# Expert picks in a two-block transformer kernel: the gathered dense part turned around on TensorE, and its masked sums moved from VectorE to TensorE

## What is computed

```python
experts = (i1 * PEER_N_KEYS + i2).reshape(T, PEER_HEADS * PEER_TOPK)
gates = jax.nn.softmax(top_vals, axis=-1).reshape(T, PEER_HEADS * PEER_TOPK)
...
u = jnp.take(expert_down, ec, axis=0)
hdn = jax.nn.gelu(jnp.einsum('ted,td->te', u, xc))
vsel = jnp.take(expert_up, ec, axis=0)
return jnp.einsum('te,ted->td', gc * hdn, vsel)
```

## Time and profile before

| what | value |
|---|---|
| median of 3 runs | 3120.47 us (3116.56 to 3124.34) |
| the profiled execution | 3122.72 us |
| its span | 3120.9 us |
| TensorE busy | 2909.6 us (93%) |
| VectorE busy | 2118.9 us (68%) |
| ScalarE busy | 1105.1 us (35%) |
| GpSimd busy | 557.2 us (18%) |
| DMA | 803.77 MB, 258 GB/s on average |
| expert stage | about 1900 us to the end |
| dense down products | 1900.2 to 2287 us |
| down rows | 1912.5 to 2576.7 us |
| tile-0 builds | from 2394 us |
| dense up products | 2651.4 to 3066 us |
| up rows | 2577.8 to 3104 us |

### The profile page before, as it was taken

One profiled execution on the slowest core, in us unless ns is written; L12 is line 12 of the kernel. 1 busy time (PEld: TensorE's weight loads), 2 busy tenths in 40 slices (PEclk: granted clock), 3 DMA queues, 4 the chain that ended last, 5 costly groups with the idle time before them and its releaser, 6 DMA issues.

```text
span 3120.9 us, 40850 instructions
## 1 busy us (share of the span) xinstructions
PE 2909.6 (93%) x16091; PEld 2422.2 (78%) x16091; DVE 2118.9 (68%) x3183; ACT 1105.1 (35%) x1716; POOL 557.2 (18%) x524
## 2 busy tenths in 40 slices
PE   7999999999999999899999999999987669999992
PEld 7999999997879987798887799888876657444441
DVE  5777777777765456744545658985578989666667
ACT  2334443444354444544444542111146757000000
POOL 0000000000000000000000002234333556544444
PEclk9899999999999999999999999999999968999996
DMA  9977777777866534465333546999966888999998
GB/s 333 338 249 255 266 259 256 261 254 239 292 199 170 156 115 148 136 197 157 114 108 114 179 159 236 316 346 407 403 245 202 276 274 302 396 410 410 410 409 308
DMA packets 359295, 803.77 MB, mean 258 GB/s; under 512 B 40152, under 2 KB 99920, under 8 KB 358336
## 3 DMA queue, kind: packets, MB, share of 16 engines
q1 hardware_dynamic: 284480, 502.08, 47.5%
q0 software_dynamic: 74624, 299.07, 25.9%
HBM read 798.96 MB, written 2.10 MB: 257 GB/s over the span
## 4 chain that ended last, share of the span: by engine, by line
PE 55%; DMA 20%; DVE 15%; issue 4%; POOL 3%; ACT 2%; SPq 0%; DVEq 0%; ACTq 0%; POOLq 0%
PE ps L1972 15%; PE ps L1974 15%; PE ps L1973 15%; DMA s<-in_up_rows,s 11%; DMA s<-in_down_rows,s 8%; DVE s L1915 5%; POOL s L701 3%; DVE s L1937 2%; PE ps L2397 1%; DVE s L1880 1%; PE ps L2016 1%; PE ps L2265 1%; DVE r L1202 1%; DMA s<-in_ada_w 1%; DVE s L1883 1%
## 5 line engine op out<-in xcount | busy, mean ns | idle before, releaser
L1972 PE MATMUL ps<-r,r 128*128 128x256 f32 (+1 forms) x3232 | 1049.6, 325 | 2.2 <-DVE r L1202 1.8
L1974 PE MATMUL ps<-r,r 128*128 128x256 f32 (+1 forms) x3232 | 1029.1, 318 | 0.0
L1973 PE MATMUL ps<-r,r 128*128 128x256 f32 (+1 forms) x3232 | 1029.0, 318 | 0.0
L1202 DVE TENSOR_TENSOR r<-s,r 128x1024 fp32r<-128x1024 f32 (+2 forms) x532 | 640.4, 1212 | 510.6 <-ACT r L716 510.2
L716 ACT CAST r<-s 128x1024 fp32r<-128x1024 f32 (+2 forms) x532 | 549.4, 1039 | 842.9 <-PE ps L1974 779.9
L1972 PEld LDWEIGHTS ps<-r,r 128*128 128x128 f32 x3232 | 622.8, 193 | 50.0 <-issue 9.2
L1973 PEld LDWEIGHTS ps<-r,r 128*128 128x128 f32 x3232 | 623.0, 193 | 43.5 <-issue 4.6
L1974 PEld LDWEIGHTS ps<-r,r 128*128 128x128 f32 x3232 | 622.0, 192 | 41.1
L1937 DVE SCALAR_TENSOR_TENSOR s<-s,s,s 128x1088 f32<-128x1088 f32 x256 | 345.8, 1351 | 162.0 <-DMA s<-in_up_rows,s 157.9
L1915 DVE CUSTOM_DVE_ANT_0 s<-s,s 128x1152 f32<-128x1152 f32 x256 | 345.0, 1353 | 108.8 <-DMA s<-in_down_rows,s 108.4
L2630 PE MATMUL ps<-s,big 128*128 128x480 f32 x1024 | 414.6, 568 | 0.0
(11 more groups left out here) (300 smaller groups left out, 2492.4 us busy)
## 6 DMA issues: line engine op xcount, KB each, us to landing
s<-in_ada_w SPq DMA_DIRECT2D x192, 512.0 KB, 5.7
s<-in_ret_w_in SPq DMA_DIRECT2D x128, 512.0 KB, 5.2
s<-in_up_blocks SPq DMA_DIRECT2D x128, 480.0 KB, 6.8
s<-in_down_blocks SPq DMA_DIRECT2D x128, 448.0 KB, 6.5
s<-in_w_in SPq DMA_DIRECT2D x96, 512.0 KB, 3.8
s<-in_ret_w_in SPq DMA_DIRECT2D x128, 256.0 KB, 4.0
s<-in_ret_w_out SPq DMA_DIRECT2D x64, 512.0 KB, 5.7
s<-in_mla_w_in SPq DMA_DIRECT2D x48, 512.0 KB, 3.7
```

Of the source, the lines that this page charges most:

```text
L1202: v.tensor_tensor(lo_of(w), raw_of(w), hi_of(w).bitcast(F), ALU.subtract).then_inc(*lo_made.to(w))
L1972: pe.matmul(o, lh, rh, start=start, stop=False, skip_group_check=True)
L1973: pe.matmul(o, lh, rl, start=False, stop=False, skip_group_check=True)
L1974: return pe.matmul(o, ll, rh, start=False, stop=stop, skip_group_check=True)
```

## The change

- DH is laid out as (i1, token) instead of four parts of (token, 32 of i1), so the dense copy is contiguous.
- `pick_rows` swaps the sides: the dense part of a token is stationary, with a step of 256 elements between its 128 columns, and PH moves. The result has i1 on partitions and the picks along the row.
- The comparison becomes four products that put the picks' i1 on all partitions, and VectorE compares them with the partition number (`POS`, a new column of the table). In tile 0 the banks 0 and 1 alternate for it; in tile 1 it is bank 1.
- The sum over i1 is now over partitions: `add_picked` makes four width-1 products of PR with a column of ones, into bank 5. The VectorE sum is gone. ScalarE copies the whole tile's sums once (`sums_copy`).
- PR has three buffers instead of two, at a new place.
- The row numbers of picks and masks change; the masks 29 to 31 of tile 0 go behind row 255, around `hidden(1)` and `coefficients(1)`.

```diff
-        PR = [sbuf[0][i][:, 0:512] for i in (2, 3)]
+        PR = [at(W + 4608 + 512 * i, 512) for i in range(3)]
...
-        PICK_AT = [146 + q // 2 for q in range(32)] + [164 + 5 * q // 2 for q in range(32)]
-        HOT_AT = [163 + 5 * (q + 3) // 2 for q in range(32)]
+        PICK_AT = [146 + 5 * q // 4 for q in range(32)] + [187 + 2 * q for q in range(32)]
+        HOT_AT = [194 + 2 * q for q in range(28)] + [251]
...
-                s.copy(DH[:, i1 // 32, :, i1 % 32:i1 % 32 + 2], bank[4 + q % 4].rearrange("p (i t) -> p t i", i=2)).then_inc(
-                    *hid_stored.to(q))
+                s.copy(flat(DH[:, i1:i1 + 2, :]), bank[4 + q % 4]).then_inc(*hid_stored.to(q))
...
-                v.scalar_tensor_tensor(out=o, in0=bank[1], scalar=0.0, in1=o, op0=ALU.is_equal,
+                v.scalar_tensor_tensor(out=o, in0=bank[1 if t else q % 2], scalar=POS, in1=o, op0=ALU.is_equal,
                                        op1=ALU.mult).then_inc(*multiplied.to((t, q)))
-                v.wait_ge(*multiplied.at((t, q)))
-                v.tensor_reduce(SL[t][:, 4 * q:4 * q + 4], o.rearrange("p (t i) -> p t i", t=4), AX.X, ALU.add).then_inc(
-                    *picked.to((t, q)))
...
             def pick_rows(t, q):
-                b = 3 + q % 2
+                b, b1 = 3 + q % 2, 1 if t else q % 2
                 take(b)
                 pe.wait_ge(*pick_hot.at((t, q)))
                 for k in range(4):
-                    c = 128 * t + 4 * q + k
-                    pe.matmul(bank[b][:, k * 128:(k + 1) * 128].rearrange("p (c i) -> p c i", c=4), PH[q % 2][:, k, :],
-                              DH[:, :, c, :], start=True, stop=True)
-                less(t, q, 0, 1).then_inc(*rows_picked.to((t, q)))
-                free[1], free[b] = multiplied.at((t, q)), rows_copied.at((t, q))
+                    pe.matmul(bank[b][:, k * 128:(k + 1) * 128], DH[:, :, 128 * t + 4 * q + k], PH[q % 2][:, k, :],
+                              start=True, stop=True)
+                take(b1)
+                for k in range(4):
+                    r = pe.matmul(bank[b1][:, k * 128:(k + 1) * 128], IDR[:, 4 * q + k:4 * q + k + 1].broadcast_to([128, 128]),
+                                  EFR[t][:, 0, :], start=True, stop=True)
+                r.then_inc(*rows_picked.to((t, q)))
+                free[b1], free[b] = multiplied.at((t, q)), rows_copied.at((t, q))
+
+            def add_picked(t, q):
+
+                pe.wait_ge(*multiplied.at((t, q)))
+                for k in range(4):
+                    r = pe.matmul(SUMS[t][:, 4 * q + k:4 * q + k + 1], PR[(32 * t + q) % 3][:, k * 128:(k + 1) * 128],
+                                  ONES[:, 0:1], start=True, stop=True)
+                r.then_inc(*picked.to((t, q)))
...
             for q in range(32):
                 if q < 31:
                     spread_(0, q + 1)
+                if q >= 2:
+                    add_picked(0, q - 2)
                 pick_rows(0, q)
             spread_(1, 0)
+            add_picked(0, 30)
...
+            first_ones(0, 29)
+            hidden(1)
+            first_ones(0, 30)
+            add_row(0)
+            first_ones(0, 31)
+            coefficients(1)
+            add_row(1)
+            add_row(2)
+            for n in range(3, 256):
+                add_row(n)
+                if n < 35:
+                    first_ones(1, n - 3)
```

More of the change, by code:

```diff
@@ L38 @@
 K_NEG = 2066
-K_ALL = 2067
+K_POS = 2067
+K_ALL = 2068
 def tables():
@@ L294, in build @@
         SQE = at(16 * KB, G2C)
-        PR = [sbuf[0][i][:, 0:512] for i in (2, 3)]
-        CO = [big.rearrange("p (c h i t) -> p c h i t", c=4, h=2, i=32)[:, :, t, :, :] for t in range(2)]
+        PR = [at(W + 4608 + 512 * i, 512) for i in range(3)]
+        CO = [DH[:, :, 128 * t:128 * (t + 1)] for t in range(2)]
         def row_slot(n):
@@ L572, in build @@
         spread, spread_read, pick_hot = sig("spread", fours), sig("spread_read", fours), sig("pick_hot", fours)
-        rows_picked, rows_copied = sig("rows_picked", fours), sig("rows_copied", fours)
+        rows_picked = sig("rows_picked", fours)
+        rows_copied = sig("rows_copied", fours[:33] + [("sum", 0)] + fours[33:] + [("sum", 1)])
         multiplied, picked = sig("multiplied", fours), sig("picked", fours)
@@ L583, in build @@
         last_root, last_made = sig("last_root", range(2)), sig("last_made", range(2))
+        SUMS = [bank[5][:, 128 * t + 128:128 * t + 256] for t in range(2)]
         BANK_OF = {(x, p): 4 + p % 2 if x == "N0" else (6, 7, 0, 1)[p] if x == "C" else p for x, p in pairs}
@@ L1104, in rows_copy, with sums_copy @@
                 s.wait_ge(*rows_picked.at((t, q)))
-                if 32 * t + q >= 2:
-                    s.wait_ge(*picked.at(fours[32 * t + q - 2]))
-                s.copy(PR[q % 2], bank[3 + q % 2]).then_inc(*rows_copied.to((t, q)))
+                if 32 * t + q >= 3:
+                    s.wait_ge(*picked.at(fours[32 * t + q - 3]))
+                s.copy(PR[(32 * t + q) % 3], bank[3 + q % 2]).then_inc(*rows_copied.to((t, q)))
+            def sums_copy(t):
+                s.wait_ge(*picked.at((t, 31)))
+                s.copy(SL[t], SUMS[t]).then_inc(*rows_copied.to(("sum", t)))
             def store(t, q):
                 s.wait_ge(*built.at((t, q)))
-                s.copy(CO[t][:, :, :, 4 * q:4 * q + 4], bank[6 + q % 2].rearrange("p (t c i) -> p c i t", t=4, c=4)).then_inc(
+                s.copy(CO[t][:, :, 4 * q:4 * q + 4], bank[6 + q % 2].rearrange("p (t i) -> p i t", t=4)).then_inc(
                     *stored.to((t, q)))
@@ L1119, in coefficients @@
                 s.wait_ge(*coef_turned.at(t))
-                s.copy(CFT[t], bank[5][:, 0:128]).then_inc(*coef_copied.to(t))
+                s.copy(CFT[t], bank[5 * t][:, 0:128]).then_inc(*coef_copied.to(t))
             def first_tile(q):
@@ L1155, in scalar @@
                 if q == 1:
+                    sums_copy(0)
+                if q == 2:
                     gelu(0)
-                if q == 3:
+                if q == 4:
                     coefficients(0)
[L1159 to L1162, removed]
+                if q >= 4:
+                    first_tile(q - 4)
+            sums_copy(1)
+            first_tile(29)
+            first_tile(30)
             gelu(1)
+            first_tile(31)
+            first_tile(32)
             coefficients(1)
@@ L1889, in hidden @@
                 v.wait_ge(*picked_turned.at(t))
-                v.tensor_tensor(HD[t], HD[t], bank[5][:, 0:128], ALU.add).then_inc(*hid_all.to(t))
+                v.tensor_tensor(HD[t], HD[t], bank[5 * t][:, 0:128], ALU.add).then_inc(*hid_all.to(t))
             def coefficients(t):
@@ L1918, in vector @@
                     gates((64, 100).index(n))
-                if n == 162:
+                if n == 188:
                     hidden(0)
-                if n == 164:
+                if n == 192:
                     coefficients(0)
-                for q in range(32):
-                    if HOT_AT[q] == n:
-                        first_ones(0, q)
+                if n in HOT_AT:
+                    first_ones(0, HOT_AT.index(n))
                 for q in range(64):
@@ L1928, in vector, with add_row @@
                         pick(*fours[q])
-            hidden(1)
-            coefficients(1)
-            for n in range(256):
+            def add_row(n):
                 t, j = n // 128, n % 128
@@ L2587, in tensor @@
             pe.wait_ge(*hid_stored.at(63))
+            take(5)
             spread_(0, 0)
```

43 lines of the change are left out of this document (23 added, 20 removed).

## The result

The changed kernel takes 3172.94 us (median of 4 runs, 3168.96 to 3182.09) against 3119.9 us before (median of 4): the ratio is 1.0173, 95% interval 1.0148 to 1.0199. It is slower by 53 us.

What follows compares the result with a forecast made beforehand. Expert stage bound by the four gather buffers in tile 0, four near-equal limits in tile 1: 3122.7 - 36.5 (row 255 sooner) + 5 (given back) = 3091.2 us; range 3076 to 3134.

Steps and rivals of the forecast that it cites:

- TensorE 2.5: Tile-0 pick on TensorE: spreads 0.39, dense products 0.88, broadcasts 0.39 and width-1 sums 0.86, together 2.5 us.
- the ring's 2.69: Tile-0 pick, limit from four gather buffers shared by rows 56 to 255: 1.25 x 2.15 = 2.69 us, taken as slowest.
- the 3 us added for the start: Rows 146 to 187: 3 us added to 88.2 because TensorE enters the stage by way of the lower clock level.
- Rival C: TensorE stays between clock levels (0.77 granted): picks 3.1 us, tile-1 pairs 4.9, row 255 at 2570, 3123 us; chance 0.08.
- Its sign for the clock: Sign that the low-clock case holds: granted clock below 0.9 in tile 1.
- the open price: Dense products' stationary load with columns 1 KB apart, 512 instructions: between 0.11 and 0.22 us each, taken at 0.11.
- By that row I take 0.11: Price per stepped load on TensorE, taken from ScalarE's stepped PSUM read (0.567 us against 0.585 in one run).
- rival A: Stepped load takes twice as long, 0.22: TensorE decides, 3.4 us a tile-0 pick, 4.8 a tile-1 pair, 3129 us; chance 0.25.
- The +5 given back: After row 255: tile 0's builds 29 to 31 come first, about 14 us instead of 9.3, so +5, bounds 0 and 6.
- ScalarE's turn: One turn of the tile-1 loop on ScalarE stays as before, 4.13 us.
- the floor: Four gather buffers limit rows to 2.15 us each; the change cannot go below; checked by one 7.06 us gather, giving 2.18.
- the 4.4 us a pair: Tile-1 pair of rows: VectorE 3.9, TensorE 3.9, ScalarE 4.13, buffers 4.3; taken as 4.4, x 32 = 140.8 us.

Runs made afterwards that it cites:

- the wide sums: Changed kernel with the four width-1 sums per pick turned around, 128 picks streaming past a stationary column of ones: 3117.38 us (median of 10), ratio 0.9992 to before.
- both removed: Changed kernel with 128-wide sums and the dense products' stationary side from 128 adjacent columns (picked values wrong): 3078.9 us, one execution.
- the first run above: Changed kernel with each dense product loading 128 adjacent columns of DH instead of columns 1 KB apart (picked values wrong): 3157.68 us, one execution.

## Why the prediction was wrong

The forecast was 3091, the measured median 3173, outside the range. Against the profiled execution the difference is 3182.1 - 3091.2 = 90.9 us, and it splits by the prediction's own steps:

| step | forecast | measured | difference |
|---|---|---|---|
| start of row 146 | 2298.3 | 2306.1 | +7.8 |
| row 146 to row 187 | 91.2 | 160.8 | +69.6 |
| row 187 to row 255 | 149.4 | 169.7 | +20.3 |
| from row 255 to the end | 552.3 | 545.5 | -6.8 |

The rows it starts from, in VectorE's timeline of the changed kernel:

```profile
2306.12 1.36 DVE L1924 CUSTOM_DVE_ANT_0 s<-s,s 128x1152 f32<-128x1152 f32 x1 [1.64 <-DMA s<-in_down_rows,s]
...
2466.95 1.35 DVE L1924 CUSTOM_DVE_ANT_0 s<-s,s 128x1152 f32<-128x1152 f32 x1
```

**Tile 0: the step that failed is "TensorE 2.5".** It stood in the sum below the ring's 2.69 and measured 5.15. All four prices were taken from rows at the full clock, and the 3 us added for the start assumed that a full engine soon runs at the full level. It ran at 0.50 for 130 us and more while it was busy without a gap. Rival C had the clock, but sized it at 0.77 and set it aside with the argument that the clock was 1.00 where the work was dense. That argument took one kind of full engine for another: the rows it rested on, 2900 to 3000 in the earlier trace rows, are products of 480 columns (250 in 100 us), while here all instructions stream 128 columns or one. Its sign for the clock ("below 0.9 in tile 1") looked at the wrong tile. That it is the clock is shown by the wide sums: equal in number, 47 us less in this stage (71 with adjacent columns) and 55 us in all.

**Tile 1: the open price was taken at the wrong end.** 0.215 instead of 0.11 an instruction, and rival A's turn of 4.8 us came out at 4.87. "By that row I take 0.11" carried ScalarE's stepped read of PSUM over to TensorE's load from SBUF. That nearest row was on another engine and another memory, and it was no evidence. By the stage table the step is worth 23 us of this stage and the shape of the sums 6, and with both removed the stage is 9 us shorter than forecast: that makes the 20.3. Rival A's 3129 was not the outcome either, since it had the full clock in tile 0. The Trainium skill (Advanced Engine Details and Errata, SBUF Cachelines) had warned of a penalty for a new 16-byte line with each access; at 2.4 GHz the traces agree, with a factor of two (0.86 to 1.72 us for eight); at 1.2 GHz they show next to none (1.70 and 1.74). Only one step was tried, 1 KB, so that the 16-byte line is the reason is not shown.

**The +5 given back** did happen where it was placed: the first tile-1 build starts 13.8 us after row 255's start (2650.4) instead of 9.3, and the dense up products 80.5 instead of 76.0 us after it (2717.1 and 2651.4). But it did not reach the end, since up rows flowed meanwhile and the rows end last. In all ten traces the part after row 255 takes 544 to 547 us.

**Right** were the removed sums on VectorE, ScalarE's turn (4.13 forecast, 4.04 in the first run above) and the tail after row 255 (547.3 us before, 545.5 after), without the 5 us added to it. **Right by luck** is how near row 255 came with the two prices set back, 2532.9 against 2538.9. In tile 0 it was not the ring of four buffers that held, as the forecast had it, but TensorE, at 2.68 us a pick and 100% busy, next to the ring's 2.69. In tile 1 a turn took 4.03 us, with no gap on ScalarE and TensorE 99% busy (49.69 of 50 us from 2450 to 2500):

```profile
2479.88 0.69 ACT L1110 ACTIVATE s<-ps,s 128x512 f32<-128x512 f32 x1
...
2483.91 0.69 ACT L1110 ACTIVATE s<-ps,s 128x512 f32<-128x512 f32 x1
```

That is 2.02 us a row, below the 2.15 that the prediction called the floor. Its check of the floor took one gather of 7.06 us; in this kernel the median gather of that stretch (2450 to 2500) landed in 5.5 us. So the ring was sized too slow, and the 4.4 us a pair with it: rows 187 to 251 took 4.11 a pair.

The start of row 146, 7.8 us later, is partly a difference between executions: the four kernels with the old copy start it between 2293.6 and 2301.4, the six with the contiguous copy between 2299.9 and 2306.1, though within each group the program is almost the same up to there. The gathers are some rows behind well before 2288. Whether the contiguous copy adds to it no run tells, and it stays open. A small miss is the mask product, 0.751 instead of 0.69 us with its scalar from a tile, 64 x 0.06 = 4 us of work on an engine that was not the bound.

**Where a gain could be had** is the other half. The kernel before gains some 24 us from the row numbers alone, once they fit its own order, most of what the prediction gave the whole change (31). Moving the sums to TensorE was not needed for it: the changed kernel stands some 80 us above that one.

## What to carry to other kernels

Before work is moved to TensorE because it has idle time, ask at which clock it will run there: TensorE stayed at half its clock for 130 us, busy without a gap, with small products. So price them at both levels, and try a sum over partitions with the wide operand moving. Price a stationary side with a step from a row that has one: at 1 KB it cost twice a packed one at the full clock. And before adding instructions, try the order alone: spreading the picks over the rows gave some 24 us, and the same spread with masks that did not fit TensorE's order cost 139.

## What the runs showed of the hardware that was not expected

- TensorE without a gap for 130 us at a granted 0.50 (2320 to 2450), and at 1.00 in the same stretch up to 2400 with as many instructions per pick, the width-1 ones made 128 wide. There the clock had come up from 0.50 (2300 to 2305) to 1.00 (from 2310). Two added 512-column products per pick raised it too, to 0.66 on average at first and to 1.00 after some 40 us.
- At 1.2 GHz a width-1 fp32 instruction, a 128-wide one, and one with a stepped stationary side take 0.21, 0.21 and 0.22 us from start to start; at 2.4 GHz they take 0.11, 0.11 and 0.215.
- A stationary side with 1 KB between its columns doubles an fp32 product of 128 columns at the full clock: 1.72 against 0.86 us for eight.
